# Prologue of a two-layer hybrid trunk: squares per landed tile, modulation rows in groups, feature tiles four by four, masks behind them

## The chip, the cores and the metric

One core of one Trainium2 chip. The metric is the device time of one execution in microseconds (us), median of the runs shown. All times of the trace count from the span's start. Engines: TensorE (PE), VectorE (DVE), ScalarE (ACT), GpSimd (POOL), SyncE (SP, which issues most DMAs).

## The reference, cut to what matters

Two layers over x (1024 tokens by 1024 channels), conditioned by a vector c; the change is in what precedes the first product of layer 0.

```python
c_act = jax.nn.silu(c)
for l in range(DEPTH):                                   # DEPTH = 2
    mod = (c_act @ w_ada[l] + b_ada[l])[:, None, :]
    sh1, sc1, g1, sh2, sc2, g2 = jnp.split(mod, N_MOD, axis=-1)
    h = rms_norm(x, norm1_g[l]) * (1.0 + sc1) + sh1
    z = h @ w_in[l]
    u, cq_in, ckv_in, kr_in, gate_a, gate_b = jnp.split(z, split_pts, axis=-1)
    y_a = s5_mixer(u, ...) @ w_a_out[l]                  # state-space scan, GLU
    y_b = mla_mixer(cq_in, ckv_in, kr_in, positions, cos, sin, ...) @ w_b_out[l]
    merged = jax.nn.sigmoid(gate_a) * y_a + jax.nn.sigmoid(gate_b) * y_b
    x = x + g1 * (merged @ w_out[l])
    h = rms_norm(x, norm2_g[l]) * (1.0 + sc2) + sh2
    x = x + g2 * ((jax.nn.silu(h @ w_gate[l]) * (h @ w_up[l])) @ w_down[l])
return rms_norm(x, final_g)
```

Attention masks by positions (key position at most query position) and rotates parts of q and k by cos and sin of the positions.

## The kernel before, in words

Every fp32 product is made of three fp32r products: high part of the weights with high part of the data, high with low, low with high (`products`, L675). A weight unit is a 128x1024 tile `raw`; ScalarE copies it to `whi` (`split_hi`, L643), GpSimd or VectorE subtracts to get `wlo` (`split_lo`, L657, the first two units on VectorE, L2499). Units live in two slots; a unit is loaded when the low part of the unit two before it is done, and split once TensorE has used that unit.

Channels are eight k-tiles of 128 (`KT`), tokens two halves of 512 (side 0 and side 1). The features h = a1 * rb * x + shift are made per k-tile and side, in the order `H_ORDER` (L700): VectorE makes the t tile (`hidden_scaled`, L2531), ScalarE its high part (`hidden_hi`, L1926), VectorE its low part (`hidden_lo`, L2541). a1 and the shift come from the modulation, rb from the norm.

The prologue of layer 0 in the old order:

- SP (L784 to L833) loads positions, c, constants, the eight tiles of x (512 KB each), then the 16 modulation row tiles (512 KB each, ring of four, two per k-tile), the first two U weight units behind row 8; then the state-space parameters.
- VectorE first makes the angles (L2451 to L2454) and the split positions; then the 16 row products (L2488), one after the other, with the rotary tables (L2475, six steps) behind row 6, the reciprocal of the root mean square of side 0 and two mask rows behind row 11, the low parts of units 0 and 1 behind rows 13 and 15. Then the bias sums and a1 for all k-tiles at once (L2502, L2505), then the features. Six more mask rows follow (L2472), then the state-space parameters' chain of small steps (L2578 on), which ends in the matrices on GpSimd (L1130 to L1136).
- ScalarE waits for all of x (L1934), squares a tile and side at a time into a ring of two per side (L1910; square k of a side waits until TensorE has consumed square k-2), with sine and half-angle sine behind the first two; side 0 first, then side 1.
- TensorE sums each square over channels with a column of 1/1024 (L1332, accumulating in one bank), then transposes and spreads the reciprocal root (`norm_scale`, L1320); ScalarE copies it to `rb` (`norm_rows`, L1921).
- TensorE then makes the 512 U columns (`u_products`, L1345): k-tiles 0 to 3 for side 0, 0 to 3 for side 1, then both sides of each further k-tile, 12 products a k-tile and side, 192 in all. Then 16 gate units of 48 products each (L1433).

Gate unit 0 writes PSUM banks 0 and 1 and waits until two u_t copies are out of them, gate unit 1 for four, its second half for eight (L1436, L1440):

```python
for t in range(2 * KT):
    unit_ready(pe, l, U_GATE + t)
    wait(pe, z_act, l, 2 * t + 2 if t < 2 else 7 + t)
```

On ScalarE the order behind the features is (L1972 to L1994): Exp of the step sizes, in layer 0 the eight mask blocks (L1957, each waits for its mask row), the high part of gate unit 0, Exp of the decay, then the eight u_t copies, with the sines of the state-space angles (L1984, they wait for VectorE's chain) behind the second copy, then the high part of gate unit 1. SP spills masks and rotary tables when all masks are done (L847), before it loads gate unit 2.

## Time and profile before

| what | value |
|---|---|
| median of 3 runs | 2959.69 us (2954.8 to 2960.44) |
| the profiled execution's own time | 2962.92 us |
| its span, first to last instruction | 2961.1 us |
| mean granted TensorE clock | 0.993 |
| TensorE busy | 2897.6 us (98% of the span) |
| VectorE busy | 2097.1 us |

The span leaves out 1.8 us around the instructions. Busy times of different engines overlap. A timeline row gives start, duration, engine, line, operation, tiles, count, and in brackets the idle time before it with what ended it; durations of TensorE rows overlap their successors, so its pace is read from starts.

### The profile page before, as it was taken

The numbers are of one execution on the slowest core, as the hardware profiler recorded it, in microseconds if no ns is written. First come the engines' busy times: TensorE is split into PE (matmuls) and PEld (weight loads), VectorE is DVE, ScalarE is ACT, GpSimd is POOL, SyncE is SP. The second block draws the span as 40 slices with busy tenths as digits, with TensorE's granted clock in tenths as the row PEclk, the third lists the DMA queues.
The fourth block names the chain that finished last, engine by engine and source line by source line (L and its number), as shares of the span: only waits on it lengthen the run. The fifth ranks groups of instructions, "written<-read, shape, count | busy, mean of one in ns | idle before, by whom it ended". The sixth has DMA issues, their size and how long they took to land.

```text
span 2961.1 us, 40255 instructions
## 1 busy us (share of the span) xinstructions
PE 2897.6 (98%) x14212; PEld 2445.4 (83%) x14212; DVE 2097.1 (71%) x2605; ACT 1148.5 (39%) x1825; POOL 1126.7 (38%) x775
## 2 busy tenths in 40 slices
PE   6999999999999999999999999999999999999998
PEld 6888889988878888888878888998887788888887
DVE  7899688865686666666668986887535776666765
ACT  3433377751242222222342336777214322222223
POOL 0355222322554444434435542232223534344343
PEclk9999999999999999999999999999999999999999
DMA  7565400225601111111144651011341111111111
GB/s 286 167 191 190 132 11 16 51 65 180 204 29 54 49 57 50 57 50 56 33 157 157 191 172 63 17 26 38 123 156 53 45 52 53 53 50 56 47 57 68
DMA packets 279184, 263.66 MB, mean 89 GB/s; under 512 B 46737, under 2 KB 237329, under 8 KB 277650
## 3 DMA queue, kind: packets, MB, share of 16 engines
q1 hardware_dynamic: 252464, 217.66, 24.1%
q10 hardware_dynamic: 26594, 44.32, 4.1%
q8 instruction: 80, 1.31, 0.2%
q14 instruction: 46, 0.38, 0.0%
HBM read 218.59 MB, written 40.96 MB: 88 GB/s over the span
## 4 chain that ended last, share of the span: by engine, by line
PE 89%; DVE 4%; ACT 3%; POOL 2%; issue 1%; DMA 1%; SPq 0%; POOLq 0%; DVEq 0%; ACTq 0%
PE ps L678 16%; PE ps L680 16%; PE ps L681 16%; PE ps L1689 9%; PE ps L1690 9%; PE ps L1691 9%; PE ps L1552 3%; PE ps L1572 2%; PE ps L1573 2%; PE ps L1533 2%; PE ps L1538 2%; PE ps L1537 2%; POOL e_lo L1266 1%; DMA ada_rows<-in_w_ada 1%; DVE h_lo L2541 1%
## 5 line engine op out<-in xcount | busy, mean ns | idle before, releaser
L625 POOL TENSOR_TENSOR wlo<-blocks,whi 128x512 fp32r<-128x512 f32 x368 | 504.5, 1375 | 729.1 <-ACT whi L619 729.1
L2984 DVE SCALAR_TENSOR_TENSOR x_sb<-ps,mod,x_sb 128x1024 f32<-128x1024 f32 x320 | 404.4, 1280 | 244.8 <-PE ps L681 237.0
L619 ACT ACTIVATE whi<-blocks 128x512 fp32r<-128x512 f32 x368 | 228.0, 629 | 761.8 <-PE ps L1691 671.3
L662 POOL TENSOR_TENSOR wlo<-raw,whi 128x1024 fp32r<-128x1024 f32 (+4 forms) x156 | 235.4, 1526 | 709.7 <-ACT whi L654 709.5
L678 PE MATMUL ps<-h_hi,whi 128*128 128x512 f32 x832 | 282.5, 402 | 10.8 <-DVE h_lo L2541 6.3
L680 PE MATMUL ps<-h_lo,whi 128*128 128x512 f32 x832 | 275.6, 394 | 0.0
L681 PE MATMUL ps<-h_hi,wlo 128*128 128x512 f32 x832 | 275.0, 393 | 0.0
L1689 PE MATMUL ps<-h_hi,whi 128*128 128x512 f32 x640 | 250.3, 391 | 3.9 <-POOL wlo L625 3.9
L1690 PE MATMUL ps<-h_lo,whi 128*128 128x512 f32 x640 | 250.2, 391 | 0.0
L1691 PE MATMUL ps<-h_hi,wlo 128*128 128x512 f32 x640 | 250.1, 391 | 0.0
L654 ACT ACTIVATE whi<-raw 128x1024 fp32r<-128x1024 f32 (+4 forms) x162 | 106.9, 699 | 349.7 <-PE ps L681 294.0
L678 PEld LDWEIGHTS ps<-h_hi,whi 128*128 128x128 f32 x832 | 155.1, 191 | 45.7 <-DVE h_lo L2541 10.7
L2402 DVE TENSOR_TENSOR pt_lo<-ps,pt_hi 128x512 fp32r<-128x512 f32 x256 | 164.5, 684 | 37.9 <-ACT pt_hi L1898 37.1
L1689 PE MATMUL ps<-e_hi,whi 128*128 128x512 f32 x480 | 187.0, 390 | 0.0
L1690 PE MATMUL ps<-e_lo,whi 128*128 128x512 f32 x480 | 186.9, 389 | 0.0
L1691 PE MATMUL ps<-e_hi,wlo 128*128 128x512 f32 x480 | 186.7, 389 | 0.0
L681 PEld LDWEIGHTS ps<-h_hi,wlo 128*128 128x128 f32 x832 | 158.1, 190 | 34.3
L680 PEld LDWEIGHTS ps<-h_lo,whi 128*128 128x128 f32 x832 | 158.2, 190 | 33.3
L1898 ACT ACTIVATE pt_hi<-ps 128x512 fp32r<-128x512 f32 x256 | 139.2, 596 | 89.7 <-PE ps L1552 88.5
L2832 DVE CUSTOM_DVE_ANT_0 ps<-ps,mask 128x1024 f32<-128x1024 f32 x128 | 157.1, 1228 | 3.3 <-issue 1.2
L1689 PEld LDWEIGHTS ps<-h_hi,whi 128*128 128x128 f32 x640 | 120.6, 188 | 29.7 <-POOL wlo L625 4.7
L2163 ACT ACTIVATE probs<-ps,neg_max 128x1024 f32<-128x1024 f32 x128 | 143.5, 1121 | 1.9 <-DVE neg_max L2832 1.8
(343 smaller groups left out, 6715.7 us busy)
## 6 DMA issues: line engine op xcount, KB each, us to landing
ada_raw<-in_w_ada SPq DMA_DIRECT2D x64, 512.0 KB, 4.6
raw<-in_w_in SPq DMA_DIRECT2D x92, 256.0 KB, 4.9
blocks<-in_w_down SPq DMA_DIRECT2D x88, 256.0 KB, 2.7
blocks<-in_w_gate SPq DMA_DIRECT2D x84, 256.0 KB, 2.9
blocks<-in_w_up SPq DMA_DIRECT2D x84, 256.0 KB, 2.9
gate_scratch<-gst ACTq DMA_DIRECT2D x32, 512.0 KB, 4.6
gl<-gate_scratch SPq DMA_DIRECT2D x32, 512.0 KB, 4.3
ada_rows<-in_w_ada SPq DMA_DIRECT2D x16, 512.0 KB, 5.7
```

Source lines behind the costliest of these rows:

```text
L619: act.activation(block_view(whi, s), blocks[:, r, :], ACT.Copy).then_inc(block_hi.sem, 1)
L625: pool.tensor_tensor(block_view(wlo, s), blocks[:, r, :], block_view(whi, s).bitcast(F32), ALU.subtract)\
L662: last = pool.tensor_tensor(dst(wlo[:, s, :]), src(raw[:, s, :]), dst(whi[:, s, :].bitcast(F32)), ALU.subtract)
L678: pe.matmul(o, w_h, x_h, start=first, stop=False)
L680: pe.matmul(o, w_h, x_l, start=False, stop=False)
L681: return [pe.matmul(o, w_l, x_h, start=False, stop=last) for o, (x_h, _) in zip(outs, xs)]
L1689: pe.matmul(bank, w_h, x_h, start=opens and j == 0, stop=False, skip_group_check=added)
L1690: pe.matmul(bank, w_h, x_l, start=False, stop=False, skip_group_check=added)
L1691: end = pe.matmul(bank, w_l, x_h, start=False, stop=(j == 3), skip_group_check=added)
L2402: return dve.tensor_tensor(out, value, hi.bitcast(F32), ALU.subtract)
L2832: dve.tensor_tensor_reduce(out=s, in0=s, in1=mask[:, step % TT, :], scale=1.0, scalar=3e38, op0=ALU.add, op1=ALU.min, accum_out=neg_max[:, ...
L2984: dve.scalar_tensor_tensor(x_sb[:, d, :], pair(banks + 2 * (d % 2)), mod[:, 5, d:d + 1], x_sb[:, d, :], ALU.mult, ALU.add).then_inc(dn_ev. ...
```

## The change

- x has one semaphore per tile. ScalarE squares each tile of side 0 as it lands and slips one square of side 1 behind each second tile (`FIRST_SQUARES`), the last four at the end; TensorE sums them in the same order, side 1 in a bank of its own, and the row scale of side 0 stands behind square 4 of side 1.
- SP issues the row tiles once the angles are ready (they now share memory with the angles' temporaries), and the four U weight units stand behind rows 4, 6, 12 and 14.
- VectorE does four row products, then modulation and a1 of k-tiles 0 and 1, their first features, four more rows for k-tiles 2 and 3, and then a group per k-tile. The low parts of units 0 and 1 come between.
- `H_ORDER` is now four k-tiles of side 0, four of side 1, then both sides of each k-tile (both layers).
- Four of the six rotary steps move to ScalarE; the other two stand before k-tile 6 on VectorE.
- All eight mask rows come behind the features; on ScalarE the high part of gate unit 0 comes before the mask blocks.
- The spill of x is issued behind the high part of U unit 2.

Left out of the diff below: where the tiles lie in SBUF, and `hidden_low` and `first_weight_lo`, which are the bodies of the old `hidden_lo` and of L2498 and L2499.

```diff
         U_FIRST = 4
-        H_ORDER = [(0, k) for k in range(5)] + [(1, k) for k in range(5)] + [(t, k) for k in range(5, KT) for t in range(2)]
+        UNIT_BEHIND_ROW = (4, 6, 12, 14)
+        FIRST_SQUARES = tuple((0, k) if t == 0 else (1, k // 2) for k in range(KT) for t in range(1 + k % 2)) + \
+            tuple((1, k) for k in range(4, KT))
+        H_ORDER = [(t, k) for t in range(2) for k in range(4)] + [(t, k) for k in range(4, KT) for t in range(2)]
...
             for k in range(KT):
-                sp.dma_start(x_sb[:, k, :], x[k * P:(k + 1) * P, :]).then_inc(x_in_loaded.sem, 16)
+                sp.dma_start(x_sb[:, k, :], x[k * P:(k + 1) * P, :]).then_inc(x_tile_loaded[k].sem, 16)
...
                 if l == 0:
+                    sp.wait_ge(angles_ready.sem, 1)
                     for n in range(2 * KT):
-                        if n == 8:
-                            for t in range(2):
-                                load_unit(sp, l, U_U + t, u_unit(t))
+                        if n in UNIT_BEHIND_ROW:
+                            t = UNIT_BEHIND_ROW.index(n)
+                            load_unit(sp, l, U_U + t, u_unit(t))
                         if n >= 4:
 
                             sp.wait_ge(rows_used.sem, n - 3)
                         k, m = divmod(n, 2)
-                        sp.dma_start(ada_rows[:, n % 4, :], w_ada[0][m * D + k * P:m * D + (k + 1) * P, :])\
+                        sp.dma_start(first_row(n), w_ada[0][m * D + k * P:m * D + (k + 1) * P, :])\
                             .then_inc(rows_loaded[n % 4].sem, 16)
                     s5_parameters(0)
-                for n in range(0 if l else 2, 4):
+                for n in range(0 if l else 4, 4):
...
+            def first_squares(half, k):
+
+                pe.wait_ge(sq_ready[half].sem, k + 1)
+                for t in range(4):
+                    last = pe.matmul(ps[:, 6 + half, t:t + 1], sq_ring[:, 2 * half + k % 2, t * P:(t + 1) * P],
+                                     mean_col[:, :], start=(k == 0 and t == 0), stop=(k == KT - 1), skip_group_check=True)
+                    if t == 2 and k == KT - 1:
                         last.then_inc(sq_added[half].sem, 1)
-                    if half and k == 3:
-                        norm_scale(0, 0)
+                if k == KT - 1:
+                    last.then_inc(sq_mm.sem, 1)
+                elif k:
+                    last.then_inc(sq_added[half].sem, 1)
+
+            for half, k in FIRST_SQUARES:
+                first_squares(half, k)
+                if (half, k) == (1, 4):
+                    norm_scale(0, 0)
...
-                    if k == 2:
+                    if k == (2 if l else 1):
...
-            act.wait_ge(x_in_loaded.sem, 16 * KT)
-            square(0, 0, 0, 0)
-            square(0, 0, 0, 1)
+            for side, k in FIRST_SQUARES:
+                if side == 0:
+                    act.wait_ge(x_tile_loaded[k].sem, 16)
+                if (side, k) == (1, 6):
+                    norm_std(0, 0)
+                square(0, 0, side, k)
+            split_hi(act, 0, U_U)
+            norm_rows(0, 0)
+            wait(act, sq_mm, 0, 2)
+            act.activation(std[:, 0, 4:8], ps[:, 7, 0:4], ACT.Sqrt, bias=eps_col[:, :]).then_inc(std_ready.sem, 1)
+            for k in range(2):
+                hidden_hi(0, 0, k)
+            split_hi(act, 0, U_U + 1)
             act.wait_ge(angles_ready.sem, 1)
             act.activation(sin_t[:, :], ang[:, :], ACT.Sin).then_inc(act_const.sem, 1)
-            act.activation(ang_k[:, :], half[:, :], ACT.Sin).then_inc(act_const.sem, 1)
-            for k in range(2, KT):
-                square(0, 0, 0, k)
-            norm_std(0, 0)
-            for k in range(4):
-                square(0, 0, 1, k)
-            split_hi(act, 0, U_U)
-            split_hi(act, 0, U_U + 1)
-            for k in range(4, 6):
-                square(0, 0, 1, k)
-            norm_rows(0, 0)
-            for k in range(6, KT):
-                square(0, 0, 1, k)
-            for k in range(3):
-                hidden_hi(0, 0, k)
+            act.activation(cos_t[:, :], half[:, :], ACT.Sin).then_inc(act_const.sem, 1)
+
+            def cosine_squares():
+
+                act.wait_ge(act_const.sem, 3)
+                act.activation(cos_t[:, :], cos_t[:, :], ACT.Square).then_inc(act_const.sem, 1)
+                act.wait_ge(act_const.sem, 4)
+                act.activation(cos_t[:, :], cos_t[:, :], ACT.Identity, scale=-2.0, bias=1.0).then_inc(act_const.sem, 1)
+
+            def cosine_tables():
+
+                act.wait_ge(act_const.sem, 5)
+                act.activation(tq[:, :], cos_t[:, :], ACT.Identity, scale=rope_sb[:, 1:2], bias=rope_sb[:, 3:4])\
+                    .then_inc(act_const.sem, 1)
+                act.activation(tk[:, :], cos_t[:, :], ACT.Copy, scale=rope_sb[:, 4:5]).then_inc(act_const.sem, 1)
+
+            cosine_squares()
+            hidden_hi(0, 0, 2)
+            norm_rows(0, 1)
+            hidden_hi(0, 0, 3)
+            cosine_tables()
 
             def mask_block(k):
                 act.wait_ge(mask_sum.sem, k + 1)
@@ -1959,22 +1986,28 @@
 
             for l in range(DEPTH):
 
-                act.dma_start(xs_dram, x_sb[:, :, :]).then_inc(x_spilled.sem, 16)
-                hidden_hi(l, 0, 3)
-                norm_std(l, 1)
-                hidden_hi(l, 0, 4)
-                norm_rows(l, 1)
-                for o, k in H_ORDER[5:]:
+                if l:
+                    act.dma_start(xs_dram, x_sb[:, :, :]).then_inc(x_spilled.sem, 16)
+                if l:
+                    hidden_hi(l, 0, 3)
+                    norm_std(l, 1)
+                    norm_rows(l, 1)
+                for o, k in H_ORDER[4:]:
                     hidden_hi(l, o, k)
-                    if (o, k) == (0, 5):
+                    if (o, k) == ((0, 5) if l else (1, 4)):
                         split_hi(act, l, U_U + 2)
-                split_hi(act, l, U_U + 3)
+                        if l == 0:
+                            act.dma_start(xs_dram, x_sb[:, :, :]).then_inc(x_spilled.sem, 16)
+                    if l == 0 and (o, k) == (1, 5):
+                        split_hi(act, l, U_U + 3)
+                if l:
+                    split_hi(act, l, U_U + 3)
                 wait(act, s5_loaded, l, 16)
                 act.activation(sm[:, S_DT, :], ldt, ACT.Exp).then_inc(s5_act.sem, 1)
+                split_hi(act, l, U_GATE)
                 if l == 0:
                     for k in range(KT):
                         mask_block(k)
-                split_hi(act, l, U_GATE)
                 wait(act, s5_dve, l, S5_EXP_READY)
...
             def rope_tables():
-                dve.wait_ge(act_const.sem, 3)
-                link(dve.tensor_tensor(ang_k[:, :], ang_k[:, :], ang_k[:, :], ALU.mult))
-                link(dve.tensor_scalar(ang_k[:, :], ang_k[:, :], -2.0, 1.0, ALU.mult, ALU.add))
-                link(dve.tensor_scalar(tq[:, :], ang_k[:, :], rope_sb[:, 1:2], rope_sb[:, 3:4], ALU.mult, ALU.add))
+                dve.wait_ge(act_const.sem, 7)
                 link(dve.scalar_tensor_tensor(tq[:, :], sin_t[:, :], rope_sb[:, 2:3], tq[:, :], ALU.mult, ALU.add))
-                link(dve.tensor_scalar(tk[:, :], ang_k[:, :], rope_sb[:, 4:5], None, ALU.mult))
                 link(dve.scalar_tensor_tensor(tk[:, :], sin_t[:, :], rope_sb[:, 5:6], tk[:, :], ALU.mult, ALU.add))
 
             dve.wait_ge(act_const.sem, 1)
-            for n in range(2 * KT):
-                k, m = divmod(n, 2)
-                dve.wait_ge(rows_loaded[n % 4].sem, 16 * (n // 4 + 1))
-                row_products(mod[:, m, k:k + 1], ada_rows[:, n % 4, :], first_c[:, :]).then_inc(rows_used.sem, 1)
-                if n == 5:
-                    rope_tables()
-                if n == 10:
-                    dve.wait_ge(std_ready.sem, 1)
-                    dve.reciprocal(rstd[:, 0, 0:4], std[:, 0, 0:4]).then_inc(rstd_ready.sem, 1)
-                    for t in range(2):
-                        mask_rows(t)
-                if n in (12, 14):
-                    t = n // 2 - 6
-                    wait(dve, w_hi_done, 0, U_U + t + 1)
-                    lo_of(wlo[:, t, :], raw[:, t, :], whi[:, t, :]).then_inc(w_lo_done.sem, 1)
-            dve.wait_ge(rows_used.sem, 2 * KT)
-            for m in range(2):
-                dve.tensor_tensor(mod[:, m, :], mod[:, m, :], cols[:, 0, ROW_B_ADA + m * KT:ROW_B_ADA + (m + 1) * KT], ALU.add)\
-                    .then_inc(mod_ready.sem, 1)
-            dve.wait_ge(mod_ready.sem, 2)
-            dve.scalar_tensor_tensor(a1[:, :], mod[:, 1, :], 1.0, cols[:, 0, ROW_N1:ROW_N1 + KT], ALU.add, ALU.mult)\
-                .then_inc(a1_ready.sem, 1)
...
+            def first_rows(ks):
+
+                for n in range(2 * ks.start, 2 * ks.stop):
+                    k, m = divmod(n, 2)
+                    dve.wait_ge(rows_loaded[n % 4].sem, 16 * (n // 4 + 1))
+                    row_products(mod[:, m, k:k + 1], first_row(n), first_c[:, :]).then_inc(rows_used.sem, 1)
+
+            def first_modulation(ks):
+
+                dve.wait_ge(rows_used.sem, 2 * ks.stop)
+                for m in range(2):
+                    bias = cols[:, 0, ROW_B_ADA + m * KT + ks.start:ROW_B_ADA + m * KT + ks.stop]
+                    sum_ = dve.tensor_tensor(mod[:, m, ks], mod[:, m, ks], bias, ALU.add)
+                    if ks.stop == KT:
+                        sum_.then_inc(mod_ready.sem, 1)
+                    else:
+                        link(sum_)
+                if ks.stop == KT:
+                    dve.wait_ge(mod_ready.sem, 2)
+                a1_part = dve.scalar_tensor_tensor(a1[:, ks], mod[:, 1, ks], 1.0, cols[:, 0, ROW_N1 + ks.start:ROW_N1 + ks.stop],
+                                                   ALU.add, ALU.mult)
+                if ks.stop == KT:
+                    a1_part.then_inc(a1_ready.sem, 1)
+                    dve.wait_ge(a1_ready.sem, 1)
+                else:
+                    link(a1_part)
+
...
+            first_rows(slice(0, 2))
+            norm_inverse(0, 0)
+            first_modulation(slice(0, 2))
             dve.wait_ge(c_stored.sem, 16)
             hidden_scaled(0, 0, 0)
-            for k in range(2):
+            hidden_lo(0, 0, 0)
+            first_weight_lo(0)
+            hidden_low(0, 1, 0)
+            norm_inverse(0, 1)
+            first_rows(slice(2, 4))
+            first_modulation(slice(2, 4))
+            hidden_scaled(0, 0, 2)
+            first_weight_lo(1)
+            hidden_lo(0, 0, 2)
+            hidden_low(0, 3, 0)
+            hidden_scaled(0, 1, 0)
+            for k in range(3):
+                hidden_lo(0, 1, k)
+            hidden_low(1, 3, 0)
+            for k in range(4, KT):
+                first_rows(slice(k, k + 1))
+                first_modulation(slice(k, k + 1))
+                if k == 6:
+                    rope_tables()
+                hidden_scaled(0, 0, k)
                 hidden_lo(0, 0, k)
+                hidden_low(1, k, 0)
             for l in range(DEPTH):
                 dve.tensor_copy(pcol[:, :], cols[:, l, :]).then_inc(pcol_ready.sem, 1)
                 wait(dve, pcol_ready, l, 1)
@@ -2560,13 +2626,15 @@
 
                 if l:
                     weight_lo(l, U_U + 1)
-                for k in range(2, 4):
-                    hidden_lo(l, 0, k)
-                norm_inverse(l, 1)
-                for o, k in H_ORDER[4:]:
-                    hidden_lo(l, o, k)
-                if l == 0:
-                    for k in range(2, KT):
+                if l:
+                    hidden_lo(l, 0, 2)
+                    hidden_low(0, 3, l)
+                    norm_inverse(l, 1)
+                    hidden_scaled(l, 1, 0)
+                    for o, k in H_ORDER[4:]:
+                        hidden_lo(l, o, k)
+                else:
+                    for k in range(KT):
                         mask_rows(k)
                     dve.wait_ge(mask_step.sem, KT)
```

## Rows read from the trace of the kernel before

**Rows 1.** Page, part 1: busy us, share of the span, instructions, by engine

```profile
PE 2897.6 (98%) x14212; PEld 2445.4 (83%) x14212; DVE 2097.1 (71%) x2605; ACT 1148.5 (39%) x1825; POOL 1126.7 (38%) x775
```

**Rows 2.** Waits of TensorE over the whole span: us in total, times, longest

```profile
PE ps L1332 <- ACT sq_ring L1910: 22.3, 4, 19.9
```

**Rows 3.** Timeline of PE, first products to first gate unit

```profile
54.24 0.79 PE L678 MATMUL ps<-h_hi,whi 128*128 128x512 f32 x1 [2.35 <-DVE h_lo L2541]
...
59.44 0.39 PE L678 MATMUL ps<-h_hi,whi 128*128 128x512 f32 x1
...
69.44 0.50 PE L678 MATMUL ps<-h_hi,whi 128*128 128x512 f32 x1 [0.71 <-DVE h_lo L2541]
...
102.21 0.62 PE L678 MATMUL ps<-h_hi,whi 128*128 128x512 f32 x2
```

**Rows 4.** Timeline of PE and ACT, squares and the row scale

```profile
24.15 10.40 PE L1332 MATMUL ps<-columns,sq_ring 128*128 128x1 f32 x48 [0.72 <-ACT sq_ring L1910]
...
31.82 1.28 ACT L1916 ACT_TABLE_LOAD   x1
...
40.15 1.99 ACT L654 ACTIVATE whi<-raw 128x1024 fp32r<-128x1024 f32 x2
...
43.22 2.05 PE L1320 MATMUL ps<-ident,rstd 128*128 128x128 f32 x8
```

**Rows 5.** Timeline of ACT's queue; line 804, landing of the x tiles

```profile
11.22 0.50 ACTq L1905 DMA_DIRECT2D c_scratch<-first_c  x1
...
L804 SPq DMA_DIRECT2D x_sb<-in_x x8: 432/508/1063, 3.1 to 7.6; - x8
...
DMA to landing us min/median/max: 6.5/8.6/11.5
```

**Rows 6.** Timeline of DVE, rows, modulation, first t tiles

```profile
20.54 1.23 DVE L2414 CUSTOM_DVE_ANT_0 ada_rows<-ada_rows,first_c 128x1024 f32<-128x1024 f32 x1 [3.14 <-DMA ada_rows<-in_w_ada]
...
34.89 1.23 DVE L2414 CUSTOM_DVE_ANT_0 ada_rows<-ada_rows,first_c 128x1024 f32<-128x1024 f32 x1
...
36.04 1.22 DVE L2414 CUSTOM_DVE_ANT_0 ada_rows<-ada_rows,first_c 128x1024 f32<-128x1024 f32 x1
...
51.41 0.24 DVE L2502 TENSOR_TENSOR mod<-mod,cols 128x8 f32<-128x8 f32 x2
...
51.89 1.42 DVE L2531 SCALAR_TENSOR_TENSOR t_ring<-x_sb,a,rb 128x512 f32<-128x512 f32 x2
```

**Rows 7.** Timeline of POOL and DVE, a GpSimd low part beside VectorE

```profile
76.41 2.52 POOL L662 TENSOR_TENSOR wlo<-raw,whi 128x1024 fp32r<-128x1024 f32 x1 [74.93 <-ACT whi L654]
...
76.97 2.51 DVE L2541 SCALAR_TENSOR_TENSOR h_lo<-t_ring,mod,h_hi 128x512 fp32r<-128x512 f32 x1 [0.30 <-ACT h_hi L1926]
...
96.93 2.80 DVE L2447 SCALAR_TENSOR_TENSOR sm<-sm 128x32 f32<-128x32 f32 x3
```

**Rows 8.** Timeline of DVE, ACT and POOL, from the masks to gate unit 1

```profile
87.12 7.49 DVE L2472 SCALAR_TENSOR_TENSOR mask_t<-pos_f,hi_bias,pos_lo 128x1024 f32<-128x1024 f32 x6 [2.78 <-ACT mask L1957]
...
95.83 0.19 DVE L2578 TENSOR_TENSOR sm<-s5p,sm 128x32 f32<-128x32 f32 x1 [1.22 <-ACT mask L1957]
...
97.71 1.22 ACT L1898 ACTIVATE u_t<-ps 128x512 f32<-128x512 f32 x2 [0.81 <-PE ps L681]
...
103.70 0.37 ACT L1984 ACTIVATE trig<-sm 128x192 f32<-128x192 f32 x1 [3.11 <-DVE sm L2587]
...
109.63 2.57 POOL L662 TENSOR_TENSOR wlo<-raw,whi 128x1024 fp32r<-128x1024 f32 x1 [10.40 <-ACT whi L654]
...
116.76 2.45 POOL L662 TENSOR_TENSOR wlo<-raw,whi 128x1024 fp32r<-128x1024 f32 x1 [4.56 <-ACT whi L654]
```

**Rows 9.** Timeline of POOL and PE, first state-space matrices and transposes

```profile
136.34 1.62 POOL L1136 TENSOR_TENSOR be<-m_tmp 128x512 f32<-128x512 f32 x1
...
140.29 0.60 PE L1385 MATMUL ps<-ident,be 128*128 128x128 f32 x4
```

**Rows 10.** Timeline of PE at the start of layer 1

```profile
1517.05 0.50 PE L678 MATMUL ps<-h_hi,whi 128*128 128x512 f32 x1 [0.70 <-DVE h_lo L2541]
```

52 lines of the change are left out of this document (25 added, 27 removed).

## Prediction

> **What bounds the kernel now.** I read the page's table of engines first: TensorE is busy for 98% of the span [rows 1], so only work that TensorE waits for can be won or lost, 63.5 us in all. The waits say where that lies: 22.3 us end on a square of x from ScalarE [rows 2], and the timeline says when. The first product starts at 54.24; a first half of the tokens for four k-tiles is done when the second half begins at 69.44, and the 144 products from there to the first gate unit at 102.21 run without a gap, 0.2276 us each [rows 3]. From there on TensorE hardly waits. The question is therefore when the first gate units run after the change, and what must be ready by then. The first twelve products stand further apart than the rest: 54.24 to 59.44 is 0.43 each, which is 512 columns at TensorE's lower level, 1.2 GHz, after an engine that had only done squares and had idled 2.35 us; from then on the spacing is that of 2.4 GHz [rows 3].
>
> **The squares.** One square tile costs TensorE eight passes (fp32, four column blocks): 48 passes in 10.40 us, so 0.217 each and 1.73 a square [rows 4]. That is slower than the tiles land (first 6.5 us after its issue at 3.08, last 11.5 after 7.62: 9.6 to 19.1, one per 1.36) [rows 5], so taking squares as the tiles land makes TensorE the bound. ScalarE is free at 11.72 [rows 5], its first square ends at about 12.4, and TensorE goes on without a gap: 11 squares (eight of side 0, three of side 1 between them) end side 0 at 12.4 + 11 x 1.73 = 31.4, two more at 34.9. The ring of two lets ScalarE square (1,5) only when (1,3) is consumed, 33.15; it ends at 33.9, then come the Sqrt table load (1.28 [rows 4]) and the root of four columns (under 0.3): 35.5. VectorE's reciprocal: 35.7. The row scale takes 2.05 at this pace [rows 4]: 37.8. Only then does TensorE take (1,5), to 39.5; square (1,7) waits for that (40.3), and behind it on ScalarE stand the high part of unit 0 (two take 1.99 [rows 4]: 41.3) and the copy of the scale (0.6, as a u_t copy of the same size, two in 1.22 [rows 8]): 41.9. The first t tile starts at 41.95 against 51.89 [rows 6]. The first product needs high part, low part and the low weights behind them: 45.9 against 54.24, **8.3 us earlier**.
>
> **VectorE until the masks.** Its start is the same: row 0 has landed at 20.5 [rows 6]; that rows are now issued at 13.6 instead of 8.2 costs nothing, since the x tiles fill the queue until 19.1 [rows 5]. But now it does four row products (to 25.4) and waits for the root, with the other twelve behind the wait. Idle to 35.5 and, after 0.65 of small work, from 36.3 to 41.95: 15.7 us, where before it did rows, tables and masks. From 41.95 on it is the bound; a row product is 1.15 (34.89 to 36.04), a t tile or low part 0.66 (two in 1.42), a low weight unit like a row product, a bias group of three linked small steps 0.65 (five more of them than before: +3.3), all of these in [rows 6], a rotary step like a mask row, 1.25 [rows 8] (two stay; four go to ScalarE, where they lie in a pause):
> t and low of (0,0), low unit 0, low (0,1): 46.5. Rows 4 to 7 with their group: 52.0. The rest of the first eight tiles, low unit 1, and 0.9 of waiting on ScalarE's rotary steps: 62.0. Each k of 4 to 7 is 2.3 + 0.65 + 2.65 = 5.6: k=4 to 67.6.
> A GpSimd low part blocks a VectorE operation: h_lo, of a t tile's size, took 2.51 beside the one begun at 76.41, and three linked steps of some 0.2 each took 2.80 at 96.93 [rows 7, 8]: about 2.0 lost each time. Units 2 and 3 now both fall among row products (before one fell into a pause): k=5 ends at 75.1, k=6 with the rotary steps at 85.3, k=7 at 90.8. Eight masks (7.49 for six, 1.25 each [rows 8], two more than before at this place) and the block by the gate unit's low part end ScalarE's last mask at **103.85**; before, VectorE went on at 95.83 [rows 8].
> Three blocks cost 6 us here; if only one of the three low units met VectorE, as before in this stretch, the sum would be 4 us less.
> The Trainium skill (SBUF — State Buffer, "SBUF: two separate sides") has a rule that speaks against this change here: a VectorE operation with two SBUF inputs and a GpSimd one lock each other out for a whole instruction. By it every one of the three low units blocks, which is the sum's 6 us. Both blocked rows agree with it.
>
> **What is late next.** TensorE finishes the U columns at about 96.2 (k=6 and k=7 paced by VectorE), 6.0 earlier than 102.21. But gate unit 0 writes banks 0 and 1, which are free after two u_t copies, and on ScalarE these now stand behind all eight masks. After the last mask: two small VectorE steps, an Exp, two copies of 1.22 together, as at 95.83 to 98.93 but without the weight split between [rows 8]: 1.95. Gate unit 0 starts at 105.8, after a wait of 9.6. It is 48 products, 10.9; after such a wait I take twelve of them at the lower level as in [rows 3], +2.4: gate unit 1 starts at **119.1**. The other condition is its low weights: at 109.63 + 2.57 = 112.2 before, 8.5 after trig at 103.70 [rows 8]. Trig comes 5.7 after the masks now (7.9 before, less the 2.15 of block that moved ahead of them): 109.6, low part 118.1. So 118.1 if TensorE stays at the upper level, 119.1 if not. Before: 102.21 + 10.9 = 113.1. The delay is 5.0 to 6.0; I take 6.0, since the row nearest to such a wait is the slow start at 54.24.
> On the clock the Trainium skill (TensorE: Matmul & The Clock Gate, "What's actually happening") says that idleness lowers it and sustained work raises it again. By it the start after the 9.6 us is slow, 6.0; without it 5.0. It also speaks of the squares, and that is a rival below.
> Behind this the state-space chain must hold: the matrices end at 136.34 + 1.62 = 138.0 before their transposes at 140.29 [rows 9], 2.3 to spare. The chain moves by 103.85 - 95.83 - 2.15 = 5.9, TensorE by 6.0: it still fits, at nothing. The raw load of gate unit 2 stands on SP behind the mask spill and moves 8, TensorE 6; its low part was done at 116.76 + 2.45 = 119.2 [rows 8] for a need at 113.1 + 10.9 = 124.0, so 2.8 remain. Row tiles 14 and 15 stand beside the 4 MB spill of x, issued near 68. At the pace of the x tiles, 8 x 1.36 = 11 us [rows 5], it is over at 79 and the rows are there before 85: nothing. At half that pace they would be there near 92 and cost up to 7. Layer 1 takes its (1,0) tile one step sooner, where TensorE waited 0.70 [rows 10]: -0.5, between 0 and -0.7.
>
> **Sum:** +6.0 - 0.5 = +5.5 us. On the profiled execution 2961.1 + 5.5 = 2966.6 of span and, with the 1.8 around it, 2968.4; that execution stands 3.2 above the median of the three runs, so the median to expect is 2959.7 + 5.5 = **2965.2**. Bounds: squares and scale +/-1, blocks -4 to +4, masks +/-1, clock -1; added up, -1.5 to +11.5.
>
> **Rivals.** (B) *Faster*: the head start carries through. TensorE ends the U columns at 96.2, and if the masks are over by 94.3 and the low weights by 107.1 (that needs the masks at 92.8), gate unit 1 starts at 107.1: -6.0, **2953.2** with layer 1. For it: the first products come 8.3 earlier, and 3.5 us of rotary work leave VectorE. Against: it needs 11 us less VectorE time than I sum; the 15.7 us of idleness are in the program's order.
> (C) *Nothing measurable*: TensorE rises to its upper level during 22 us of unbroken squares. The same eight-pass row scale took 2.05 after squares; at twice the pace squares keep up with the tiles, the first t tile comes some 8 us sooner, the masks end near 96, gate unit 1 starts near 111: -2, **2957.5**. Against it: 10.40 us of unbroken passes show 0.217 throughout, and the next row scale is still slow [rows 4]. The Trainium skill's page on the clock gate, named above, would have it happen, with 2957.5 as its result; the trace of before does not agree.
> (D) *Slower still*: row tiles 14 and 15 land after VectorE asks for them at 85.3, because the spill of x now runs beside them. Every us that they are late moves k-tile 7, the masks and gate unit 0: 5 us late gives +10.5, **2970**; 7 gives 2972. For it: the spill is issued just before them. Against it: the 6 us between the spill's end at the tiles' pace and the need.
> That the change does not do what it says can be in one point: if the x tiles land nearly together instead of one by one, squares can't begin at 11.7; their spacing is worked out from first and last alone, and this would add to A.
>
> **How the numbers follow.** A measurement tells about 0.2%, 5.9 us, from no change. My forecast (A) has 0.64; centred at +5.5 and spread by the blocks and the clock, it holds 0.34 within 5.9 and 0.30 above. B 0.14, C 0.11 (all within), D 0.11 (above). Faster 0.14, same 0.45, slower 0.41. The range takes in A's bounds, C and part of D, and leaves B and D's end out: 2956 to 2971.
>
> **What would show it.** Right: first t tile near 42 and first product near 46; passes of the squares at 0.217 with no long pause from 12.4 to 35; VectorE idle about 10 us before the first reciprocal; a TensorE wait near 10 us ended by u_t copies just before gate unit 0, at about 106; gate unit 1 at about 119. Wrong: square passes near 0.11 (C); last mask before 95 (B); rows as releasers of VectorE, or a raw load as releaser of ScalarE near 120 (D); any change beyond the first 150 us other than layer 1's half microsecond.

## The result, and the profile after

| | before | after |
|---|---|---|
| median of six runs, us | 2959.53 (2954.8 to 2961.44) | 2974.02 (2972.06 to 2977.86) |
| ratio, 95% interval | | 1.0051 (1.0041 to 1.0061) |
| profiled execution, span | 2961.1 | 2972.1 |
| mean granted TensorE clock | 0.993 | 0.991 |

The kernel is slower by 0.5%, 15 us by the ratio. The forecast was 2965.2 us within 2956 to 2971, so the sign was right, the size was not, and the time lies 3 us above the range. In the tables below each ratio is to the kernel before as measured beside that kernel (medians 2957.2 to 2959.5 us). One of the eleven executions of a later variant, e2_l1_new, took 10339 us and is in no ratio.

**Squares to first product.** Timelines of TensorE, then of VectorE, in the kernel after (start, duration, engine, line, operation, tiles, count, idle time before and its releaser):

```profile
10.98 22.32 PE L1341 MATMUL ps<-columns,sq_ring 128*128 128x1 f32 x104 [10.98 <-ACT sq_ring L1921]
34.09 2.08 PE L1332 MATMUL ps<-ident,rstd 128*128 128x128 f32 x8 [0.80 <-DVE rstd L2558]
...
44.06 0.77 PE L686 MATMUL ps<-h_hi,whi 128*128 128x512 f32 x1 [2.98 <-DVE wlo L2435]
```

```profile
33.86 0.18 DVE L2558 RECIPROCAL rstd<-std 128x4 f32<-128x4 f32 x1 [9.91 <-ACT std L1927]
...
39.91 1.42 DVE L2570 SCALAR_TENSOR_TENSOR t_ring<-x_sb,a,rb 128x512 f32<-128x512 f32 x2 [5.44 <-ACT rb L1909]
```

104 passes in 22.32 us are 0.215 each, as in [rows 4]. By its pace, 22 us without a pause did not bring TensorE to its upper level: the row scale behind them takes 2.08, and the same eight passes in layer 1 take 1.05.

```profile
1515.27 1.05 PE L1332 MATMUL ps<-ident,rstd 128*128 128x128 f32 x8
```

The granted clock does not show this. It reads 1.00 from 11 to 33 us, and 1.00 also from 44 to 50 us, where the first products stand 0.43 apart; so at the start of the execution the level is read from the pace alone. The first t tile comes at 39.91 (before 51.89 [rows 6]), the first product at 44.06 (before 54.24 [rows 3]). In front of that t tile VectorE idles 9.91 and 5.44 us.

**VectorE until the masks, and gate unit 0.** GpSimd's rows, what stood beside them on VectorE, then the masks and what TensorE waited for, all of the kernel after:

```profile
67.78 3.11 POOL L670 TENSOR_TENSOR wlo<-raw,whi 128x1024 fp32r<-128x1024 f32 x1 [66.30 <-ACT whi L662]
81.10 2.37 POOL L670 TENSOR_TENSOR wlo<-raw,whi 128x1024 fp32r<-128x1024 f32 x1 [10.21 <-ACT whi L662]
```

```profile
68.59 3.38 DVE L2447 CUSTOM_DVE_ANT_0 row_pair<-row_pair,first_c 128x1024 f32<-128x1024 f32 x1
...
81.10 3.57 DVE L2570 SCALAR_TENSOR_TENSOR t_ring<-x_sb,a,rb 128x512 f32<-128x512 f32 x2
...
94.74 9.39 DVE L2505 SCALAR_TENSOR_TENSOR mask_t<-pos_f,hi_bias,pos_lo 128x1024 f32<-128x1024 f32 x6 [0.15 <-ACT mask L1984]
105.35 0.19 DVE L2646 TENSOR_TENSOR sm<-s5p,sm 128x32 f32<-128x32 f32 x1 [1.21 <-ACT mask L1984]
```

```profile
107.16 1.19 PE L686 MATMUL ps<-h_hi,whi 128*128 128x512 f32 x2 [8.08 <-ACT u_t L1909]
...
147.27 0.60 PE L1396 MATMUL ps<-ident,be 128*128 128x128 f32 x4
```

A row product takes 3.38 instead of 1.22, two t tiles 3.57 instead of 1.42, six masks 9.39 instead of 7.49: each GpSimd low part cost VectorE about 2 us. VectorE's next chain of small steps starts at 105.35 (before 95.83 [rows 8]), gate unit 0 at 107.16 after a wait of 8.08 (before 102.21 without one [rows 3]), the first state-space transposes at 147.27 (before 140.29 [rows 9]): **+7.0 us** in layer 0.

TensorE's pace behind such waits is in the windows (busy time and count of PE, PEld, DVE, ACT, POOL, granted clock, DMA share, GB/s), kernel after:

```profile
80.00:100.00 20.00, 15.01 (x58) 11.56 (x56) 19.40 (x22) 10.35 (x12) 5.46 (x2) 0.91 0.41 142
100.00:120.00 20.00, 12.84 (x48) 10.46 (x49) 17.32 (x53) 11.99 (x17) 2.57 (x1) 0.83 0.70 252
120.00:140.00 20.00, 20.00 (x90) 16.55 (x89) 19.03 (x47) 5.35 (x5) 5.62 (x2) 1.00 0.79 258
```

VectorE is busy 19.4 of the 20 us before the last masks, while TensorE idles, and the granted clock falls to 0.83 around the 8 us wait, to be at 1.00 again behind it.

**Start of layer 1.** GpSimd, VectorE and TensorE in the kernel after, behind the first t tiles of side 1:

```profile
1527.04 10.49 POOL L670 TENSOR_TENSOR wlo<-raw,whi 128x1024 fp32r<-128x1024 f32 x2 [18.52 <-ACT whi L662]
```

```profile
1526.49 0.75 DVE L2577 SCALAR_TENSOR_TENSOR h_lo<-t_ring,mod,h_hi 128x512 fp32r<-128x512 f32 x1
1527.16 0.75 DVE L2570 SCALAR_TENSOR_TENSOR t_ring<-x_sb,a,rb 128x512 f32<-128x512 f32 x1
...
1531.13 0.75 DVE L2570 SCALAR_TENSOR_TENSOR t_ring<-x_sb,a,rb 128x512 f32<-128x512 f32 x1
1531.79 3.50 DVE L2577 SCALAR_TENSOR_TENSOR h_lo<-t_ring,mod,h_hi 128x512 fp32r<-128x512 f32 x2
```

```profile
1534.89 0.77 PE L686 MATMUL ps<-h_hi,whi 128*128 128x512 f32 x1 [4.33 <-POOL wlo L670]
1535.45 0.63 PE L688 MATMUL ps<-h_lo,whi 128*128 128x512 f32 x1
```

In the first of these rows two low parts, of U units 2 and 3, take 10.49 us together; the first is the longer one, 7.7, where one alone takes 2.4. GpSimd's line in this stretch (duration in ns: min, median, max; first and last start):

```profile
L670 POOL TENSOR_TENSOR wlo<-raw,whi x2: 2819/5262/7705, 1527.0 to 1534.7; 128x1024 fp32r<-128x1024 f32 x2
```

TensorE waits 4.33 us for the first, then makes seven products about 0.43 apart. In the kernel before the same low part took 2.52 beside a VectorE operation of 2.51, as in [rows 7], and TensorE did not wait for it:

```profile
1524.03 2.52 POOL L662 TENSOR_TENSOR wlo<-raw,whi 128x1024 fp32r<-128x1024 f32 x1 [16.82 <-ACT whi L654]
```

```profile
1524.59 2.51 DVE L2541 SCALAR_TENSOR_TENSOR h_lo<-t_ring,mod,h_hi 128x512 fp32r<-128x512 f32 x1 [0.31 <-ACT h_hi L1926]
```

**Where the time went.** The line of the state-space transposes gives the first and last start; the first product after the last residual tile marks the start of layer 1. Kernel before, then after:

```profile
L1385 PE MATMUL ps<-ident,be x64: 270/272/276, 140.3 to 1769.4; 128*128 128x128 f32 x64
```

```profile
1503.04 0.71 PE L678 MATMUL ps<-h_hi,whi 128*128 128x512 f32 x1 [2.29 <-DVE x_sb L3082]
```

```profile
L1396 PE MATMUL ps<-ident,be x64: 270/272/276, 147.3 to 1777.8; 128*128 128x128 f32 x64
```

```profile
1504.35 0.50 PE L686 MATMUL ps<-h_hi,whi 128*128 128x512 f32 x1 [2.29 <-DVE x_sb L3150]
```

Up to the first transposes +7.0; from there to layer 1, which the change doesn't touch, 1362.7 became 1357.1, -5.7; from there to the last transposes 266.4 became 273.4, **+7.1**; the rest +2.6. The sum is the +11.0 between the spans. In all fourteen kernels profiled here the untouched stretch lies between 1356.3 and 1362.7 us, with before at the upper end, so its -5.7 is scatter between executions, and so may be the +2.6 of the rest, which no kernel changed either and which lies between 1186.7 and 1194.3. The two touched stretches make 14.1, beside the 15 of the ratio.

Not all of layer 1's 7.1 is the change's. TensorE has two more waits there, in the kernel after:

```profile
1510.98 0.79 PE L686 MATMUL ps<-h_hi,whi 128*128 128x512 f32 x1 [1.35 <-DVE h_lo L2577]
...
1519.35 0.50 PE L686 MATMUL ps<-h_hi,whi 128*128 128x512 f32 x1 [0.28 <-DVE h_lo L2577]
```

Behind the first the products stand 0.43 apart until 1513.7, six of them, with a granted clock of 0.50 from 1511 to 1514. The second is the wait of [rows 10]: 0.28 instead of 0.70.

### The profile page after: what moved, and what is told of

It reads as the page before. It is cut to its first block, busy times and chain, and to the rows that moved or that the text cites. A ratio compares the mean times of both kernels' runs of the same rounds, so it can differ in the third digit from the quotient of the medians.

```text
span 2972.1 us, 40280 instructions
## 1 busy us (share of the span) xinstructions
PE 2901.6 (98%) x14212; PEld 2447.7 (82%) x14212; DVE 2098.6 (71%) x2616; ACT 1152.7 (39%) x1830; POOL 1135.5 (38%) x775
## 4 chain that ended last, share of the span: by engine, by line
PE 88%; DVE 5%; ACT 3%; POOL 2%; issue 1%; DMA 0%; SPq 0%; POOLq 0%; ACTq 0%; DVEq 0%
PE ps L686 15%; PE ps L688 15%; PE ps L689 15%; PE ps L1700 9%; PE ps L1702 9%; PE ps L1701 8%; PE ps L1563 3%; PE ps L1583 2%; PE ps L1584 2%; PE ps L1544 2%; PE ps L1549 2%; PE ps L1548 2%; DVE h_lo L2577 1%; POOL e_lo L1278 1%; PE ps L1341 1%
## 5 line engine op out<-in xcount | busy, mean ns | idle before, releaser
L670 POOL TENSOR_TENSOR wlo<-raw,whi 128x1024 fp32r<-128x1024 f32 (+4 forms) x156 | 243.4, 1577 | 711.7 <-ACT whi L662 711.6
L686 PEld LDWEIGHTS ps<-h_hi,whi 128*128 128x128 f32 x832 | 155.5, 192 | 65.2 <-issue 19.4
```

Of the source, the lines that this page charges most:

```text
L670: last = pool.tensor_tensor(dst(wlo[:, s, :]), src(raw[:, s, :]), dst(whi[:, s, :].bitcast(F32)), ALU.subtract)
L686: pe.matmul(o, w_h, x_h, start=first, stop=False)
```

## The experiments

The two stretches are read in every run as above. GpSimd's column is the time of unit 2's low part in layer 1. The last three columns come from one profile each. In the four kernels whose layer 0 is the same (after, e1_l1_old, e3_l1_low_dve, e11_pause) the first transposes lie between 146.9 and 148.5, and 107.1 to 107.7 us behind the first t tile.

| kernel | ratio to before (95%) | first transposes | layer 1's stretch | GpSimd |
|---|---|---|---|---|
| before | 1 | 140.3 | 266.4 | 2.5 |
| after | 1.0051 (1.0041 to 1.0061) | 147.3 | 273.4 | 7.7 |
| e1_l1_old | 1.0033 (1.0020 to 1.0046) | 148.5 | 267.8 | 2.5 |
| e2_l1_new | 1.0016 (1.0007 to 1.0025) | 140.6 | 275.7 | 7.7 |
| e3_l1_low_dve | 1.0022 (1.0013 to 1.0031) | 146.9 | 266.0 | on VectorE |
| e11_pause | 1.0022 (1.0009 to 1.0035) | 147.1 | 267.4 | 2.5 |
| e4_rows_ahead | 1.0016 (1.0005 to 1.0026) | 145.4 | 266.4 | 2.5 |
| e5_copies_ahead | 1.0039 (1.0026 to 1.0053) | 151.0 | 265.9 | on VectorE |
| e6_two_mask_rows | 1.0015 (1.0005 to 1.0024) | 145.0 | 266.0 | on VectorE |
| e7_lows_dve | 1.0014 (1.0005 to 1.0023) | 146.1 | 267.3 | on VectorE |
| e8_side0_first | 1.0000 (0.9991 to 1.0009) | 141.5 | 266.0 | on VectorE |
| e9_scalar_order | 0.9993 (0.9984 to 1.0003) | 139.8 | 266.0 | on VectorE |
| e10_gate_ahead | 0.9999 (0.9987 to 1.0011) | 141.1 | 266.1 | on VectorE |
| e12_all | 0.9985 (0.9972 to 0.9997) | 135.9 | 267.3 | on VectorE |

### Layer 1: is it the order of the features, and why

**e1_l1_old**: the kernel after, with layer 1's features in the old order.

```diff
-        H_ORDER = [(t, k) for t in range(2) for k in range(4)] + [(t, k) for k in range(4, KT) for t in range(2)]
+        H_ORDERS = ([(t, k) for t in range(2) for k in range(4)] + [(t, k) for k in range(4, KT) for t in range(2)],
+                    [(0, k) for k in range(5)] + [(1, k) for k in range(5)] + [(t, k) for k in range(5, KT) for t in range(2)])
...
             for l in range(DEPTH):
+                H_ORDER[:] = H_ORDERS[l]
...
                     norm_std(l, 1)
+                    hidden_hi(l, 0, 4)
                     norm_rows(l, 1)
...
-                    hidden_low(0, 3, l)
+                    hidden_lo(l, 0, 3)
                     norm_inverse(l, 1)
-                    hidden_scaled(l, 1, 0)
```

> The changed kernel with layer 1's feature tiles in their old order (five of side 0, five of side 1, then in turn); layer 0 stays changed. Theory 1, the measured +14.5 us is two halves, +7.0 in layer 0's prologue and +7.1 where layer 1 begins, and the second is the order: some 2967 us, 7.5 over the kernel before, TensorE's waits at the start of layer 1 as before and no wait of 4.3 us for the low part of U unit 2. Rival, layer 1's loss is TensorE's clock or chance and not the order: 2974 us, the waits still there.

**e2_l1_new**: the other half, the kernel before with the new order in layer 1 alone.

> The kernel before with only layer 1's feature tiles in the new order. Theory 1: +7, 2966.5 us, with a GpSimd low part of U unit 2 of 7 us and a TensorE wait of 4 us behind it. Rival, the order matters only together with the changed prologue or not at all: 2959.5 us.

Measured: 2969.28 and 2964.98 us beside 2958.75 of before. The stretch of layer 1 is at 267.8 with the old order in the kernel after, and at 275.7 with the new one in the kernel before. The order alone costs 5.6 us of that stretch in the one pair and 9.3 in the other, whatever the prologue is, where I had forecast a gain of half a microsecond. (By the ratio e2_l1_new is 4.7 us slower, 2.1 to 7.4.) Part of the 9.3 is the clock: behind the same wait of 1.35 us e2_l1_new has twelve products 0.43 apart, the kernel after six. GpSimd's row in e2_l1_new is that of the kernel after:

```profile
1525.41 10.48 POOL L662 TENSOR_TENSOR wlo<-raw,whi 128x1024 fp32r<-128x1024 f32 x2 [19.95 <-ACT whi L654]
```

**e3_l1_low_dve**: the kernel after; in layer 1 VectorE makes unit 2's low part itself, behind the features of (1,5), and GpSimd waits for it and starts with unit 3:

```diff
-                for n in range(U_U + 2, ahead + 1):
+                if l:
+                    wait(pool, w_lo_done, l, U_U + 3)
+                    apart(pool)
+                for n in range(U_U + (3 if l else 2), ahead + 1):
                     column_lo(n)
...
                     for o, k in H_ORDER[4:]:
                         hidden_lo(l, o, k)
+                        if (o, k) == (1, 5):
+                            weight_lo(l, U_U + 2)
```

> The changed kernel, but in layer 1 the low part of U unit 2 is made by VectorE behind the sixth k-tile's features instead of by GpSimd. Theory 1a, back-to-back VectorE operations keep GpSimd from that low part: the wait of 4.3 us and the slow products behind it (2.4) go, 2974 - 6.7 = 2967.5 us. Rival 1b, the low part is late because its high part is: TensorE waits as long for VectorE's, 2974 us.

Measured 2965.42 us; the stretch falls to 266.0, that of before, with the new order in place. So the order as such costs nothing; the low part on GpSimd does, and it could still be slow for a reason other than VectorE.

**e11_pause**: the kernel after; VectorE stands still once, until GpSimd is done.

```diff
                     for o, k in H_ORDER[4:]:
                         hidden_lo(l, o, k)
+                        if (o, k) == (0, 5):
+                            wait(dve, w_lo_done, l, U_U + 3)
+                            apart(dve)
```

> The kernel after, with one wait more: in layer 1 VectorE stops behind the low part of (0,5) until GpSimd has the low weights of unit 2. Theory (VectorE's unbroken run of two-input operations keeps GpSimd out; it lost 5 us there, and TensorE behind it): the GpSimd operation takes 2.5 us instead of 7.7, VectorE stands still for some 2.5, TensorE's wait of 4.3 us falls below 1.5 and the stretch from the first product on the new x_sb to the last state-space transpose is 266 to 269 us instead of 273.4; time near 2967. Rival (the operation is slow for another reason, as the loads beside it, or the pause costs as much): it stays above 5 us, or the stretch at 272 or more, time near 2974.

Measured 2966.64 us, stretch 267.4. GpSimd's and VectorE's timelines in e11_pause:

```profile
1530.50 2.46 POOL L670 TENSOR_TENSOR wlo<-raw,whi 128x1024 fp32r<-128x1024 f32 x1 [18.48 <-ACT whi L662]
```

```profile
1529.96 0.74 DVE L2577 SCALAR_TENSOR_TENSOR h_lo<-t_ring,mod,h_hi 128x512 fp32r<-128x512 f32 x1
1533.11 0.75 DVE L2570 SCALAR_TENSOR_TENSOR t_ring<-x_sb,a,rb 128x512 f32<-128x512 f32 x1 [2.40 <-POOL wlo L670]
```

With a pause of 2.40 us on VectorE the low part takes 2.46 instead of 7.7, TensorE's wait is gone, and the stretch is 6.0 shorter. The loads and every other operation are those of the kernel after, in the same order. That leaves VectorE's unbroken run of two-input operations as the cause. Both e3_l1_low_dve and e11_pause stand at 1.0022, 6.5 us, which is about layer 0's 7.0 alone.

### Layer 0: what sets the first transposes

**e4_rows_ahead**: e1_l1_old, with twelve row products instead of four ahead of the first reciprocal, and one bias group for them.

```diff
-            first_rows(slice(0, 2))
+            first_rows(slice(0, 6))
             norm_inverse(0, 0)
-            first_modulation(slice(0, 2))
+            first_modulation(slice(0, 6))
...
```

> As the first of these, and VectorE makes twelve row products, not four, before the first reciprocal, with one bias group for k-tiles 0 to 5. Theory 2, layer 0 loses by VectorE's idle time before its first t tile: eight products (9.2 us) move into it and three bias groups of 0.65 go, the masks end near 94.3 instead of 105.35, gate unit 1 starts near 108.5 instead of 113.1 in the kernel before: 2955 us. Rival, the rows land too late to fill that time, or TensorE and ScalarE set the pace: the first t tile moves later by what the products take, 2967 us or more.

Measured 2962.82 us, transposes at 145.4, where the theory had 2955 us and the masks' end near 94.3: it failed. VectorE in e4_rows_ahead:

```profile
38.97 0.17 DVE L2570 RECIPROCAL rstd<-std 128x4 f32<-128x4 f32 x1
...
45.02 1.41 DVE L2582 SCALAR_TENSOR_TENSOR t_ring<-x_sb,a,rb 128x512 f32<-128x512 f32 x2 [5.36 <-ACT rb L1918]
...
58.40 0.75 DVE L2589 SCALAR_TENSOR_TENSOR h_lo<-t_ring,mod,h_hi 128x512 fp32r<-128x512 f32 x1 [2.86 <-ACT h_hi L1946]
```

The row products fill the idle 9.9 us, but hold the reciprocal back from 33.9 to 39.0, since their tiles land only between 26 and 38; the 5.36 behind it stays, and VectorE now waits for h_hi of ScalarE, 2.60 us up to 54.8 and 2.86 up to 58.4. Of 15 us of idleness 2.5 were won at the start of VectorE's chain (102.86 for 105.35).

**e5_copies_ahead**: e3_l1_low_dve, with two u_t copies ahead of the mask blocks on ScalarE. **e6_two_mask_rows**: besides e3_l1_low_dve, VectorE's part of six mask blocks left out, so that ScalarE makes these blocks from old data. **e7_lows_dve**: besides e3_l1_low_dve, layer 0's three low parts of this stretch on VectorE.

> The kernel after with unit 2 of layer 1 split on VectorE (the kernel of the run that gave 2965.4 us, first transposes at 146.9), and in layer 0 ScalarE makes its first two u_t copies ahead of the eight masks. Theory (VectorE's chain through masks and state-space matrices sets the end of this stretch, the 8.1 us wait for u_t is only where it shows): gate unit 0 starts near 99 instead of 107, the wait comes back ahead of gate unit 1 or of the transposes, these stay at 146 to 148, and the time at 2964 to 2967. Rival (the copies behind the masks are what costs): transposes near 140, time near 2959.

> The same base; VectorE's part of six of the eight mask blocks is left out (ScalarE still does its eight steps on old data). It takes 6 x 1.25 = 7.5 us from VectorE, but ScalarE's eight steps of 1.1 then end near 101.3 instead of 105.3. Theory (VectorE's chain is the bound of layer 0): first transposes 4 us earlier, near 143, and the time near 2961.5. Rival (TensorE's waits and slow starts come from elsewhere): transposes at 146 to 147, 2965.

> The same base; the low parts of units 2 and 3 and of gate unit 0 in layer 0 are made by VectorE instead of GpSimd. Theory (a GpSimd low part costs VectorE what it waits beside it, 2.15, 2.15 and 1.9 us in the trace after, 6.2 in all, more than the 3 x 1.15 = 3.5 of doing it): masks end 2.8 us earlier, transposes near 144, time near 2962.5. Rival (the long VectorE operations are not caused by GpSimd and remain): VectorE gets 3.5 us more, transposes near 150, 2969.

Measured 2968.16, 2961.31 and 2961.43 us beside 2965.42 of e3_l1_low_dve. The intervals of these ratios overlap that of e3_l1_low_dve, so the readings rest on one profile each. In e5_copies_ahead gate unit 0 does start at the end of the U columns, and the wait comes back, longer, at gate unit 1; waits of TensorE from 80 to 160 us (total, times, longest):

```profile
PE ps L686 <- POOL wlo L670: 11.3, 1, 11.3
PE ps L686 <- DVE h_lo L2589: 4.1, 1, 4.1
```

The high part of gate unit 1 stands on ScalarE behind masks, Sin and copies, so its low part is done at 120.9. So the 8.1 us at u_t were a symptom, and the transposes came at 151.0, not at the 146 to 148 I had written: both conditions of gate unit 1 hang on the end of the masks, and the one left was later.

In e6_two_mask_rows VectorE's chain starts at 102.10, 3.2 earlier than in the kernel after although its first t tile came 1.2 later (41.07); with that taken off it is 4.4 for 4 expected. The transposes came 1.9 earlier than in e3_l1_low_dve, at 145.0 instead of 143: the later start takes 1.2, and from gate unit 0 (103.91) to them TensorE took 41.1 instead of 40.1. In e7_lows_dve the chain starts at 104.49 with a first t tile 1.6 later than in the kernel after (41.49): 2.4 us won between them, for 2.8 expected, and the later start hides most of it at the transposes (146.1). Counted from the first t tile, the transposes come 103.9 us later in e6_two_mask_rows and 104.6 in e7_lows_dve, for 107.1 in e3_l1_low_dve: 3.2 and 2.5 less, beyond the 0.6 of scatter. A blocked operation cost VectorE more (2 us) than doing GpSimd's work (1.14).

**e8_side0_first**: e3_l1_low_dve, side 0's eight squares first, its root and row scale right behind them. Besides, some of the first high parts stand between side 1's squares, row groups are taken earlier, and the row scale of side 1 comes one k-tile earlier; the diff shows the order of the squares and the row scale.

```diff
-        FIRST_SQUARES = tuple((0, k) if t == 0 else (1, k // 2) for k in range(KT) for t in range(1 + k % 2)) + \
-            tuple((1, k) for k in range(4, KT))
+        FIRST_SQUARES = tuple((t, k) for t in range(2) for k in range(KT))
...
-                if (half, k) == (1, 4):
+                if (half, k) == (1, 0):
                     norm_scale(0, 0)
...
```

> The same base; all eight squares of side 0 go before those of side 1, the first root follows them at once, two more row groups are taken early, the row scale of side 1 comes after the first k-tile. Theory (VectorE's 15 us of idleness before its first t tile come from the root being behind eleven squares): root at 26.5 instead of 33.9, first t tile at 29.5 instead of 39.9, masks over by 88 to 93 instead of 105, then the stretch is no longer paced by VectorE alone: transposes at 130 to 139, time 2949 to 2958. Rival (the idleness only moves, because rows arrive between 26 and 39 and ScalarE is late with h_hi): masks over near 100, transposes near 143, time near 2962.

Measured 2957.44 us, the ratio exactly 1. VectorE's timeline:

```profile
26.39 0.18 DVE L2563 RECIPROCAL rstd<-std 128x4 f32<-128x4 f32 x1 [2.31 <-ACT std L1952]
30.47 1.41 DVE L2575 SCALAR_TENSOR_TENSOR t_ring<-x_sb,a,rb 128x512 f32<-128x512 f32 x2 [1.04 <-ACT rb L1911]
...
57.69 0.75 DVE L2582 SCALAR_TENSOR_TENSOR h_lo<-t_ring,mod,h_hi 128x512 fp32r<-128x512 f32 x1 [6.96 <-ACT h_hi L1939]
...
99.34 0.19 DVE L2657 TENSOR_TENSOR sm<-s5p,sm 128x32 f32<-128x32 f32 x1 [1.22 <-ACT mask L1989]
```

The root comes at 26.4 as expected and the first t tile at 30.5 instead of 39.9. Of the idle 15.4 us ahead of it 3.4 are left, so most of them were those of the squares' order. 7 us are lost again behind ScalarE's sines, and VectorE's chain starts at 99.3, with the masks' end forecast at 88 to 93. The transposes come at 141.5 instead of 130 to 139; that the time still lies within 2949 to 2958 does not bear the theory out.

**e9_scalar_order** and **e10_gate_ahead** take ScalarE's part of e8_side0_first in turn: sines and cosine squares into its own wait ahead of side 1's row scale; then, besides, two copies and gate unit 1's high part ahead of the masks, and Sin behind the sixth copy (the second diff).

```diff
-            norm_rows(0, 1)
             act.wait_ge(angles_ready.sem, 1)
             act.activation(sin_t[:, :], ang[:, :], ACT.Sin).then_inc(act_const.sem, 1)
...
             cosine_squares()
-            cosine_tables()
+            norm_rows(0, 1)
...
+                    if l == 0 and (o, k) == (1, 3):
+                        cosine_tables()
```

```diff
                 split_hi(act, l, U_GATE)
                 if l == 0:
+                    wait(act, x_spilled, l, 16)
+                    for n, (ct, side) in enumerate(U_ORDER[0:2]):
+                        wait(act, u_mm, l, n + 1)
+                        copy(u_t[:, ct, half_cols(side)], ps[:, U_BANK[ct][side], :]).then_inc(z_act.sem, 1)
+                    split_hi(act, l, U_GATE + 1)
...
                     for k in range(KT):
                         mask_block(k)
...
-                    if n == 2:
+                    if n < 2 and l == 0:
+                        continue
+                    if n == (2 if l else 6):
                         wait(act, s5_dve, l, S5_ANGLES_READY)
...
```

> The kernel with side 0's squares first (2957.4 us, masks over at 99.3, first transposes at 141.5), in which VectorE waited 7.0 us for h_hi of (1,0) behind ScalarE's sines and cosine steps. Here sines and cosine squares fill ScalarE's own 6 us wait ahead of the row scale of side 1, and the cosine tables come behind h_hi of (1,3). Theory (VectorE is still the bound): masks over at 93 to 95, transposes at 135 to 137, time near 2952. Rival (the wait is found again at the next ScalarE result, or another bound takes over): masks over after 97, transposes after 139, time 2956 or more.

> The same, and ScalarE makes two u_t copies and the high part of gate unit 1 ahead of the masks, and the Sin of the state-space angles behind the sixth copy. Theory (with copies alone ahead, gate unit 1's low weights, 121 us, became the bound; with its high part ahead too, only VectorE's matrices hold the transposes): gate unit 0 starts when the U columns end, near 90, gate unit 1 without a wait, transposes at 132 to 134, time near 2950. Rival (masks and Sin pushed back cost as much as is won, as in the run with the copies ahead): transposes at 137 or later, time 2954 or more.

Measured 2956.66 and 2956.96 us. In e9_scalar_order VectorE's chain starts at 96.95, 2.4 earlier, and the transposes come at 139.8, where the rival had them: 3.9 us were lost at 64.2 behind the high part of unit 2, which itself waited 4.3 for TensorE. In e10_gate_ahead ScalarE waits for the end of the U columns with the masks behind it; they end 5.4 later (chain at 102.34), and TensorE stops for the weights of gate unit 2:

```profile
104.16 0.69 PE L686 MATMUL ps<-h_hi,whi 128*128 128x512 f32 x2 [3.07 <-ACT u_t L1911]
...
122.89 1.22 PE L686 MATMUL ps<-h_hi,whi 128*128 128x512 f32 x2 [7.57 <-POOL wlo L670]
```

Its rival had this right: what goes ahead of the masks pushes them.

**e12_all**: e9_scalar_order, unit 2's high part one tile later, the two copies behind the fifth mask step, gate unit 1's high part behind the fourth copy, Sin behind the sixth.

> The kernel with side 0's squares first and the sines early (masks over at 96.95, gate unit 0 at 98.77, first transposes at 139.8, ratio 0.9993), with ScalarE's high part of unit 2 one tile later (VectorE waited 3.9 us behind it), its first two u_t copies behind the fifth mask step instead of ahead of or behind all eight, the high part of gate unit 1 behind the fourth copy and Sin behind the sixth. Theory (VectorE's chain of masks and matrices, 40 us from the end of the masks to the first matrix, is what is left, and nothing but its start moves the transposes now): masks over at 95 to 97, gate unit 0 at 91 to 93, first transposes at 135.5 to 137.5, time near 2953.5. Rival (copies in the middle hold up the masks as whole groups did, or TensorE's start sets the transposes): masks over after 98, transposes at 139 or later, time 2956 or more.

Measured 2954.17 us beside 2957.16 of before, ratio 0.9985 (0.9972 to 0.9997): some 4 us faster than the kernel before, 1 to 8 by the interval, which ends just below 1 and is that of the best of several variants. Against the kernel after (1.0051) it is clearly faster. Timeline of TensorE:

```profile
91.47 0.70 PE L686 MATMUL ps<-h_hi,whi 128*128 128x512 f32 x2 [1.23 <-ACT u_t L1911]
...
116.65 1.22 PE L686 MATMUL ps<-h_hi,whi 128*128 128x512 f32 x2 [3.13 <-POOL wlo L670]
...
135.93 0.60 PE L1398 MATMUL ps<-ident,be 128*128 128x128 f32 x4
```

The chain starts at 94.90, gate unit 0 at 91.47 behind a wait of 1.23, and the transposes come at 135.93. Each is within 0.1 us of where the theory put it. But the theory had nothing but VectorE left, and TensorE also waits 3.13 for gate unit 2, whose raw load stands on SP behind the spill of the masks. The first matrix is done at 134.9 (133.29 + 1.62), so without that wait the gain would be 1 us at most.

## Why the prediction was wrong

**The step that failed** is the one sentence on layer 1: "Layer 1 takes its (1,0) tile one step sooner, where TensorE waited 0.70: -0.5, between 0 and -0.7." The gain it names did come: that wait fell to 0.28. What the term left out is GpSimd's low part of unit 2, which came 5 us late; TensorE waited 4.33 for it and made its next products slowly, and the stretch became 7.1 longer. The extra tile of lead took away the 0.31 us for which VectorE had waited for ScalarE. Without this pause VectorE ran its two-input operations back to back from 1518.54 to 1531.79, and the low part that began at 1527.04 came through only where the run ended; there it held the last of them up by 2 us. e2_l1_new shows the cost without the prologue, e11_pause shows the cause. That a pause as short as 0.31 is enough was not tested by itself: it rests on the three kernels with the old order (before, e1_l1_old, e4_rows_ahead), where the low part came in at pauses of 0.31 to 0.34 and took 2.5, beside the two with the new order and no pause, where it took 7.7.

I had bounded the step by the wait I saw on TensorE, and had priced meetings of the two engines in one direction alone, GpSimd holding up VectorE. Nor had I any rival for it: all three lay in layer 0. The prediction's own sign of being wrong, a change beyond the first 150 us other than half a microsecond, is what came.

Some 6 of the 7.1 are the low part: the kernel after has 273.4, e11_pause 267.4, e1_l1_old 267.8, and in all three the products behind the 1.35 us wait (1510.98 in the kernel after) stand 0.43 apart. The rest, 1.3 or so, is this slow start, and it is the clock's and not the order's: with it the stretch is 267.3 to 267.8 where the block is absent (e1_l1_old with the old order; e7_lows_dve, e11_pause and e12_all with the new), without it 265.9 to 266.4 (before and e4_rows_ahead with the old; the others with the new). Like with like, the new order without the block is some 0.4 shorter than the old, about the gain forecast.

The Trainium skill (SBUF — State Buffer, "SBUF: two separate sides") states that of a VectorE operation with two SBUF inputs and a GpSimd one that reads SBUF, whichever starts first gets the port pair that they share for its whole instruction, and the other blocks. The blocks of 2 us in layer 0 agree with it. At 1527.04 it leaves open what happened: GpSimd came while a VectorE operation ran, and at its end the next VectorE operation went first, eight times in a row, each at the usual pace of 0.66. In layer 0 GpSimd got in after one VectorE operation (it came at 67.78, the row product at 68.59 is the one held up); there a read of the accumulator of 0.08 stands between two row products. Its third low part came at 93.75, and the masks from 94.74 on, behind a pause of 0.15, are the ones held up. By the rule, read as turns, the low part of unit 2 would have waited for one operation and cost VectorE 2 us; it waited for eight more, and the measurement decides. Why the next VectorE operation goes first there stays open.

**Layer 0** was right in mechanism and near in size: +7.0 for +6.0.
- Squares at 0.215 each, for 0.217. Start at 10.98 instead of 12.4, reciprocal at 33.9 for 35.7, first t tile at 39.9 for 41.95, first product at 44.1 for 45.9.
- VectorE from its first t tile to the start of the chain: 65.4 us for 61.9. 1.6 of the 3.5 fell in the first eight tiles (a wait of 1.53 for h_hi among them); k-tiles 4 to 7 took 30.3 for 28.8, each 0.2 to 0.5 longer; the masks 13.5 for 13.05.
- Three blocks of 2.15, 2.15 and 1.9, where I counted three of 2.0. e7_lows_dve bears them out.
- Chain at 105.35 for 103.85; end of the U columns at 99.1 for 96.2; gate unit 0 at 107.2 for 105.8, its wait 8.1 for 9.6; gate unit 1 at 120.1 for 119.1. The slow pace cost 2.0 (40.1 from gate unit 0 to the transposes, 38.1 before) for 2.4.
- That copies behind the masks were not the bound by themselves stood in the sum as the second condition, the low weights of gate unit 1 at 118.1 beside 119.1; they came at 119.6. e5_copies_ahead shows the bound.

Rival C, TensorE at its upper level in the squares, did not come: 22.32 us of unbroken passes stayed at 0.215, and the row scale at 2.08. (Its 2957.5 also leaves out layer 1's half microsecond.) By the Trainium skill (TensorE: Matmul & The Clock Gate, "What's actually happening") sustained work raises the clock; for these passes the trace, by its pace, does not agree. Rival D, late rows, did not come: VectorE waited for no row after 20 us in the kernel after. Rival B needed 11 us less of VectorE; e8_side0_first, e9_scalar_order and e12_all found 6, 8.4 and 10.5 of them by other orders, with all the masks made.

## What to carry to other kernels

An idle gap on one engine can be what lets another run: before taking a short wait out of a back-to-back run of VectorE operations with two SBUF inputs, look for a GpSimd operation that gets in there, and who waits for it. Price moves that look free on every engine that gets in their way, in both directions, and in every layer that the order applies to, not only where the change is aimed. When a wait of the busiest engine is near its source in several conditions, moving the one that is named shows only the next (8.1 us at u_t, 11.3 at the weights, 7.6 at gate unit 2); shorten what they all hang on.

## What the runs showed that I had not expected

- A GpSimd subtraction of 128x1024 took 7.7 us beside an unbroken run of VectorE operations of 0.66 us each, 2.46 with VectorE stopped. In layer 0, where row products, small steps and waits stand between, the same operation took 2.4 to 3.1 and VectorE lost 2 us.
- Moving the low part onto VectorE, which takes 1.14 us there from start to start, was cheaper than either engine's loss (e3_l1_low_dve, e7_lows_dve).
- A stretch of some 1360 us that no kernel here changed differed by up to 6.4 us between profiled executions, more than several of the effects sought. Single profiles had to be compared stretch by stretch; their spans alone would have put the change at 11.
